# Weight blocks of 256 columns stored at a pitch of 264 elements in SBUF

## The reference, cut to what matters

```python
def conv_ffn(h, w_up, conv_w, conv_b, w_down):
    u = h @ w_up
    ...
    gate, val = jnp.split(u, 2, axis=-1)
    return (jax.nn.silu(gate) * val) @ w_down

def swiglu(h, w13, w2):
    a, b = jnp.split(h @ w13, 2, axis=-1)
    return (jax.nn.silu(a) * b) @ w2
```

## Time and profile before

| | |
|---|---|
| median of 3 runs | 3395.38 us (3394.8 to 3398.59) |
| the profiled execution | 3398.26 us |
| its span, first to last instruction | 3396.5 us |
| mean granted TensorE clock | 0.991 of full speed |
| busy: PE, PEld, DVE, ACT, POOL | 97%, 83%, 53%, 36%, 31% |
| DMA | 402.66 MB, mean 119 GB/s |

### The profile page before, as it was taken

The page is one execution under the profiler, slowest core; times in us unless marked ns, Lnnn a source line. Parts: engine busy times, 40 slices in busy tenths (PEclk is TensorE's granted clock), DMA queues, the critical chain, the costliest instruction groups (busy, mean ns, idle before and its releaser), DMA issues.

```text
span 3396.5 us, 48090 instructions
## 1 busy us (share of the span) xinstructions
PE 3308.1 (97%) x17856; PEld 2820.7 (83%) x17856; DVE 1790.4 (53%) x2205; ACT 1223.1 (36%) x1582; POOL 1041.1 (31%) x513
## 2 busy tenths in 40 slices
PE   7989999999989999999999999999999999999999
PEld 7768888888878888998888877988888888988887
DVE  5465876543368856457655556664552245262222
ACT  4344433343344423543322346422242223442221
POOL 2111222211112222554444232343423332233332
PEclk9989999999999999999999999999999999999999
DMA  4212433321214433444544220454432243213222
GB/s 149 75 38 75 150 141 119 129 89 50 87 63 161 144 117 111 171 171 173 198 167 167 108 96 8 146 194 148 164 110 91 95 167 112 100 64 110 94 92 99
DMA packets 69900, 402.66 MB, mean 119 GB/s; under 512 B 7520, under 2 KB 10096, under 8 KB 31088
## 3 DMA queue, kind: packets, MB, share of 16 engines
q1 hardware_dynamic: 46400, 318.79, 26.1%
q10 hardware_dynamic: 23344, 81.73, 6.7%
HBM read 398.39 MB, written 2.10 MB: 118 GB/s over the span
## 4 chain that ended last, share of the span: by engine, by line
PE 90%; DVE 3%; ACT 2%; issue 2%; POOL 1%; DMA 1%; SPq 0%; DVEq 0%; ACTq 0%; POOLq 0%
PE banks L509 23%; PE banks L510 23%; PE banks L511 23%; PE banks L420 3%; PE banks L421 3%; PE banks L422 3%; PE banks L526 2%; PE banks L528 2%; PE banks L527 2%; ACT whi L925 1%; PE banks L579 1%; POOL wlo L2143 1%; DMA raw<-stream 1%; PE banks L837 1%; PE banks L850 1%
## 5 line engine op out<-in xcount | busy, mean ns | idle before, releaser
L2143 POOL TENSOR_TENSOR wlo<-raw,whi 128x512 fp32r<-128x512 f32 x283 | 718.8, 2540 | 2003.5 <-ACT whi L925 1989.3
L509 PE MATMUL banks<-h_hi,whi 128*128 128x512 f32 (+1 forms) x2752 | 1042.6, 379 | 14.4 <-POOL wlo L2143 7.3
L510 PE MATMUL banks<-h_lo,whi 128*128 128x512 f32 (+1 forms) x2752 | 1034.2, 376 | 0.0
L511 PE MATMUL banks<-h_hi,wlo 128*128 128x512 f32 (+1 forms) x2752 | 1034.1, 376 | 0.0
L925 ACT ACTIVATE whi<-raw 128x2048 fp32r<-128x2048 f32 x281 | 536.9, 1911 | 527.4 <-PE banks L511 523.9
L1441 DVE TENSOR_TENSOR wlo<-raw,whi 128x1536 fp32r<-128x1536 f32 x281 | 521.6, 1856 | 304.7 <-ACT whi L925 304.4
L509 PEld LDWEIGHTS banks<-h_hi,whi 128*128 128x128 f32 x2752 | 518.4, 188 | 115.4 <-issue 20.4
L510 PEld LDWEIGHTS banks<-h_lo,whi 128*128 128x128 f32 x2752 | 518.5, 188 | 95.6 <-issue 3.3
L511 PEld LDWEIGHTS banks<-h_hi,wlo 128*128 128x128 f32 x2752 | 518.5, 188 | 93.9
L509 PE MATMUL banks<-mid_hi,whi 128*128 128x512 f32 (+1 forms) x1136 | 424.6, 374 | 6.3 <-POOL wlo L2143 5.2
L510 PE MATMUL banks<-mid_lo,whi 128*128 128x512 f32 (+1 forms) x1136 | 423.7, 373 | 0.0
(11 more groups left out here) (274 smaller groups left out, 4008.9 us busy)
## 6 DMA issues: line engine op xcount, KB each, us to landing
raw<-stream SPq DMA_DIRECT2D x299, 1024.0 KB, 4.8
mraw<-mod_stream ACTq DMA_DIRECT2D x144, 512.0 KB, 3.3
x<-xT SPq DMA_DIRECT2D x8, 256.0 KB, 5.3
out<-x SPq DMA_DIRECT2D x8, 256.0 KB, 2.1
ka<-k_a ACTq DMA_DIRECT2D x1, 1600.0 KB, 7.4
ko<-k_odd ACTq DMA_DIRECT2D x1, 1152.0 KB, 5.1
crow<-c_rows ACTq DMA_DIRECT2D x1, 1024.0 KB, 6.6
cx<-ctxT SPq DMA_DIRECT2D x1, 1024.0 KB, 7.6
```

The lines of the kernel that those rows point to most:

```text
L509: mm(o, hi, a_hi[:, kc, 0:T], start=(kc == 0), stop=False)
L510: mm(o, hi, a_lo[:, kc, 0:T], start=False, stop=False)
L511: last = mm(o, lo, a_hi[:, kc, 0:T], start=False, stop=(kc == K - 1))
L2143: G.tensor_tensor(wlo[:, slot, WD:], raw[:, slot, WD:], whi[:, slot, WD:].bitcast(F32), ALU.subtract)\
```

## The change

In both slots of `whi` and `wlo` the eight blocks of a slab stand 264 elements apart (1056 bytes) instead of 256 (1024 bytes). The tiles grow from 2 x 2048 to 2 x 2112 elements, 256 elements more in all, and `PAD_MID` is smaller by 256. All that reads or writes these tiles goes by blocks: `blocks` and `raw_blocks` give the eight rows of 256. `raw` stays as it is, and `xhi` and `xlo` keep a pitch of 256. The number of instructions, matmuls, waits and DMAs stays the same. Lines of the same kind elsewhere (`split_extra`, the first two slabs, `slab_tokens`, `halved`) are changed alike and are left out here.

```diff
@@ -94,7 +94,8 @@
-PAD_MID = 456
+PITCH = 264
+PAD_MID = 200
...
@@ -192,8 +193,8 @@
         raw = sb("raw", [P, 2, SLAB])
-        whi = sb("whi", [P, 2, SLAB], F32R)
-        wlo = sb("wlo", [P, 2, SLAB], F32R)
+        whi = sb("whi", [P, 2, 8 * PITCH], F32R)
+        wlo = sb("wlo", [P, 2, 8 * PITCH], F32R)
...
@@ -338,11 +339,18 @@
+        def blocks(w):
+
+            return w.rearrange("p (k n) -> p k n", k=8)[:, :, 0:256]
+
+        def raw_blocks(slot):
+            return raw[:, slot].rearrange("p (k n) -> p k n", k=8)
+
         def w_hi(s):
-            return xhi[:, EXTRA[s]] if s in EXTRA else whi[:, s % 2]
+            return blocks(xhi[:, EXTRA[s]] if s in EXTRA else whi[:, s % 2])
 
         def w_lo(s):
-            return xlo[:, EXTRA[s]] if s in EXTRA else wlo[:, s % 2]
+            return blocks(xlo[:, EXTRA[s]] if s in EXTRA else wlo[:, s % 2])
...
@@ -413,7 +421,7 @@
             def w_tile(w, slot, kc, j, n=P):
-                return w[:, slot, kc * 256 + j * P:kc * 256 + j * P + n]
+                return w[:, slot, kc * PITCH + j * P:kc * PITCH + j * P + n]
...
@@ -425,8 +433,8 @@
                 for j in js:
-                    w = slice(kc * 256 + j * P, kc * 256 + (j + 1) * P)
-                    last = three(half_cols(order, acc[s % 2][j], at), h[:, w], lo[:, w],
+                    w = slice(j * P, (j + 1) * P)
+                    last = three(half_cols(order, acc[s % 2][j], at), h[:, kc, w], lo[:, kc, w],
...
@@ -922,7 +930,7 @@
-                    A(whi[:, s % 2, :], raw[:, s % 2, :], ACT.Copy).then_inc(whi_done, 1)
+                    A(blocks(whi[:, s % 2]), raw_blocks(s % 2), ACT.Copy).then_inc(whi_done, 1)
...
@@ -1431,15 +1439,15 @@
-            WD = SLAB - WPOOL
+            WD = 8 - WPOOL // 256
...
-                    V.tensor_tensor(wlo[:, s % 2, 0:WD], raw[:, s % 2, 0:WD], whi[:, s % 2, 0:WD].bitcast(F32),
-                                    ALU.subtract).then_inc(wlo_done, 1)
+                    V.tensor_tensor(blocks(wlo[:, s % 2])[:, 0:WD], raw_blocks(s % 2)[:, 0:WD],
+                                    blocks(whi[:, s % 2])[:, 0:WD].bitcast(F32), ALU.subtract).then_inc(wlo_done, 1)
...
@@ -2140,12 +2149,14 @@
-                G.tensor_tensor(wlo[:, slot, WD:], raw[:, slot, WD:], whi[:, slot, WD:].bitcast(F32), ALU.subtract)\
+                G.tensor_tensor(blocks(wlo[:, slot])[:, WD:], raw_blocks(slot)[:, WD:],
+                                blocks(whi[:, slot])[:, WD:].bitcast(F32), ALU.subtract)\
                     .then_inc(wlo_pool_done, 1)
```

## The result

The changed kernel took 3450.78 us in the median of four runs (3450.0 to 3452.21) against 3395.2 us before: a ratio of 1.0163, with a 95% interval of 1.0151 to 1.0175. That is 55.6 us more, slower, and 9 us beyond the upper end of the range. The profiled execution has a span of 3450.4 us, 53.9 more than before.

The account below looks back on a forecast made before the run. PE was taken to bound the kernel, a count of matmuls times their spacing. The terms 0 (a) + 0.9 (b) + 0 (c), on a median of 3395.4 us, gave 3396.0 us, in a range of 3320 to 3442.

Parts of the forecast that it names:

- Part (a): Addresses of PE's weight reads: new block places leave matmul spacing unchanged, 0 us, with bounds of -148 to +44 us.
- the evenness of the earlier trace: Settled 512-column stretch: weights alternate between column offsets and blocks, and the spacing of 226.7 ns doesn't follow them.
- the case of `hc`: `hc_hi` and `hc_lo`, not at a multiple of 512 bytes from the weights: starts jitter, but the mean stays 120.0 ns.
- second rival: Moving blocks breaks a lock between PE's weight and moving reads: 4.4 ns on 10080 matmuls, +44 us, 3440 us; chance 0.16.
- Part (b): Row breaks when ACT, DVE and POOL split a slab: mostly hidden, +0.9 us in PE's waits, at most +3.8 us.
- Part (c): Position of what lies behind `whi`: `PAD_MID` keeps `mid_hi`, `cx`, `xhi` and `xlo` in place, 0 us.
- first rival: The 13.3 ns surplus per matmul is a read clash that shifted blocks escape: 3321 us (chance 0.14) or 3247 us (0.07).
- the 227.4 ns that the text set: Mean spacing of 512-column matmuls from which the broken lock would decide, 7 us over 10080 matmuls.
- The rule of the Trainium skill: PE's SBUF read ports for the moving operand and LDWEIGHTS are independent, so placement should never matter.
- The 215.8 ns: Skill's figure for a warm 512-column matmul, 512/2.4 + 2.5; against the trace's 226.7 it left some 11 ns unexplained.

Follow-up runs that it names:

- place: Changed kernel with the blocks of `whi` and `wlo` back to 256 apart, slots still 2112 elements and everything behind them left in place: 3393.89 us.
- shift8: Changed kernel with pitch back at 256 and a pad of 8 elements below `whi`, so all weights move by 32 bytes: 3455.44 us.
- comove: Changed kernel, pitch 264 kept, with the chunks of `h_hi` and `h_lo` 520 elements apart instead of 512: 3426.11 us.
- h_shift8: Changed kernel with pitch 256; `h_hi` and `h_lo` moved by 32 bytes, the weights by 256 bytes, `mid` left in place: 3432.55 us.
- lo_shift8: Changed kernel with pitch 256 and a pad of 8 elements between `whi` and `wlo`, so only `wlo` moves by 32 bytes: 3458.89 us.
- all8: Changed kernel with pitch 256 and a pad of 8 elements below `h_hi`, so `h`, the weights and `mid` all move by 32 bytes: 3397.3 us.
- shift16: Changed kernel with pitch 256 and a pad of 16 elements below `whi`, so all weights move by 64 bytes: 3454.48 us.

## Why the prediction was wrong

**What bounds the kernel** was read rightly: a count of matmuls times their spacing, with 13 us for each ns. The whole loss is in that product.

**Part (a), 0 us, is the step that failed.** It rested on the earlier trace rows and on the evenness of the earlier trace rows. The evenness proves nothing, since every offset in it, block to block and half to half, is a multiple of 256 bytes, and these are all the same offset, as `place` showed. And the case of `hc` has 256 columns, where an offset costs nothing in any run: with all weights off by 32 bytes (`shift8`) the 512-column matmuls lose 6.7 ns, and those of 256 columns gain 1.5. The price at 512 columns can't be read from 256. By the code `hc_hi` stands 13536 - 456 = 13080 elements behind `mid_hi`'s place, 96 bytes over a multiple of 256, and that distance was never measured at 512 columns. Nor can the duration of LDWEIGHTS show the price: for the loads of `whi` and `wlo` beside `h` its mean is 188 ns before, in the changed kernel and in `shift8`. What the same rows did show, a jitter where all aligned cases are even, was named in the second rival and given 0.16.

**Part (b)** was right in size: 3 ns for ACT's seven breaks where 5 were forecast, 0 for DVE, 10 to 16 for POOL inside the bound of 204, and +2.4 us of waits where 0.9 stood and 3.8 was the bound. **Part (c)**, 0 us, was right: `place`, and `xhi` untouched.

**The first rival**, a clash that the shift relieves, had the pair of reads right and the sign wrong at 512 columns.

**The second rival** had the side, and its mechanism half. The loss is in PE's settled spacing at 512 columns, and it passed the 227.4 ns that the text set. The price, taken from the nine matmuls of the earlier trace rows at 231.1 ns, was 4.4 ns; 5.9 was measured, +59.5 us instead of +44, and that is why 3442 was too low an end. What it said of the cause, that the lock breaks because the offset changes each time, was wrong as the whole cause: `shift8` is even again, with steps of 232 to 235 ns, and is slower than the changed kernel. The offset itself costs. Where the offset does change, the steps of `comove` show such a broken stretch beside it.

**The rule of the Trainium skill** ("SBUF — State Buffer", "Who interferes with whom"), by which PE's two read ports are independent, would have given no change. `shift8` and `h_shift8` show 6.7 ns a matmul for the distance between just these two operands, so the measurement decides against it for float32r matmuls with a new weight tile each. The 215.8 ns that the prediction took from "TensorE: Matmul & The Clock Gate" of the Trainium skill ("Back-to-back issue gap") are, by that section, the gap of an isolated matmul and not that of a stream of loads and matmuls as here, so the 11 ns above it don't say what the surplus is.

What stays open: by what the two reads meet. 226.7 and 233.3 ns are 512 + 32 and 512 + 48 cycles at 2.4 GHz, whole numbers, which looks like a count of lost cycles for each load; this is argued from the numbers alone. Constant distances of 16, 96 and 160 bytes weren't tried at 512 columns, so one of them may be better than 0.

## What to carry to other kernels

Where PE is the bound and every matmul of 512 float32r columns loads new weights, keep the weights and the moving rows at the same address modulo 256 bytes, block for block; here a pad that breaks this cost up to 2.9% of the spacing, 1.6% of the time in the changed kernel and 1.9% in `lo_shift8`. Moves by multiples of 256 bytes (`place`) and of all together (`all8`) cost nothing here. And when a trace looks as if addresses didn't matter, first work out which remainders its addresses cover, and at which length of matmul.

## What the runs showed that was not expected

The same distance has opposite effects at two lengths: 32 and 64 bytes cost 6.7 ns at 512 columns and gain 1.5 and 3.5 ns at 256 (`shift8`, `shift16`). One tile in three out of place (`lo_shift8`, 233.3 ns) costs as much as all three. And 192 bytes costs 2.2 ns where its neighbours 128 and 224 cost 5.7 and 6.7.
